# Branches A and B of a hybrid encoder layer: values with v stationary and channels first, probabilities divided by their sum ahead of their transposes

## The reference

```python
def hybrid_layer(x, ...):
    h = rms_norm(x, norm_g)
    proj = jnp.einsum('bsd,de->bse', h, w_in) + b_in          # split into the operands of A, B, C and gates
    y_a = indexer_sparse_attention(a_q, a_k, a_v, i_q, i_k, i_w)   # 8 heads, 2 of k and v, of 64; top 128 keys of an indexer
    y_b = chunked_relpos_attention(b_q, b_k, b_v, rel_bias)        # 8 heads of 64, chunks of 64 tokens, learned bias
    y_c = mlstm_chunkwise(...)                                     # 4 heads of 128
    ...
    branches = jnp.stack([y_a * silu(a_z), y_b * silu(b_z), y_c * silu(c_z)], axis=2)
    y = jnp.einsum('bsnw,nwd->bsnd', branches, w_branch)
    merged = jnp.sum(sigmoid(gates) * y, axis=2)
    return x + jnp.einsum('bsd,de->bse', merged, w_out)
```

```python
p = jax.nn.softmax(s, axis=-1)        # s: scores with mask or bias
o = jnp.einsum('bhqk,bkhd->bqhd', p, v)
```

## Time and profile before

| | |
|---|---|
| Median of three runs | 1332.26 us (1331.98 to 1332.41) |
| Profiled execution, its own time | 1330.72 us |
| Profiled execution, span | 1328.9 us |
| PE busy | 1287.5 us, 97% |
| PE weight loads busy | 1080.2 us, 81% |
| DVE busy | 714.4 us, 54% |
| ACT busy | 621.8 us, 47% |
| POOL busy | 610.0 us, 46% |
| Mean granted clock of TensorE | 0.996 of full |

### The profile page before, as it was taken

The page is one execution under the profiler, slowest core; times in us unless marked ns, Lnnn a source line. Parts: engine busy times, 40 slices in busy tenths (PEclk is TensorE's granted clock), DMA queues, the critical chain, the costliest instruction groups (busy, mean ns, idle before and its releaser), DMA issues.

```text
span 1328.9 us, 19950 instructions
## 1 busy us (share of the span) xinstructions
PE 1287.5 (97%) x6525; PEld 1080.2 (81%) x6525; DVE 714.4 (54%) x1444; ACT 621.8 (47%) x1119; POOL 610.0 (46%) x767
## 2 busy tenths in 40 slices
PE   5999999999999999999999999999999999999997
PEld 3788888888987888887878888888888878888876
DVE  5678888856347112112657897977544532121155
ACT  4444666776444323333344456577754333323332
POOL 3556333342224555545765543334321545455472
PEclk9999999999999999999999999999999999999998
DMA  5322211222132233333142221112213222322321
GB/s 182 144 89 93 95 49 51 77 73 71 34 127 65 83 100 101 95 101 104 66 175 94 96 96 64 48 58 86 64 49 111 80 80 87 103 95 87 103 95 63
DMA packets 37030, 117.39 MB, mean 88 GB/s; under 512 B 4064, under 2 KB 6496, under 8 KB 36448
## 3 DMA queue, kind: packets, MB, share of 16 engines
q1 hardware_dynamic: 34368, 111.37, 25.2%
q10 hardware_dynamic: 2592, 5.11, 1.2%
HBM read 110.18 MB, written 6.29 MB: 88 GB/s over the span
## 4 chain that ended last, share of the span: by engine, by line
PE 81%; DVE 10%; ACT 4%; issue 3%; POOL 1%; DMA 0%; ACTq 0%; DVEq 0%; SPq 0%; POOLq 0%
PE acc L591 65%; PE ps_o L704 4%; PE ps_t L691 3%; DVE score L1179 1%; PE ps_t L682 1%; PE ps_o L711 1%; PE ps_s L661 1%; DVE top L1178 1%; PE ps_s L667 1%; DVE att_c L1311 1%; POOL w_lo L540 1%; DVE ak_s L1152 1%; PE spare L643 1%; ACT prob L937 1%; PE ps_s L675 1%
## 5 line engine op out<-in xcount | busy, mean ns | idle before, releaser
L540 POOL TENSOR_TENSOR w_lo<-w_raw,w_hi 128x256 fp32r<-128x256 f32 x752 | 598.7, 825 | 687.2 <-ACT w_hi L786 687.2
L591 PE MATMUL acc<-h_hi,w_hi 128*128 128x512 f32 x1136 | 454.2, 400 | 0.3 <-ACT w_hi L786 0.3
L591 PE MATMUL acc<-h_lo,w_hi 128*128 128x512 f32 x1136 | 445.4, 392 | 0.0
L591 PE MATMUL acc<-h_hi,w_lo 128*128 128x512 f32 x1136 | 297.1, 395 | 2.1 <-POOL w_lo L540 2.1
L786 ACT ACTIVATE w_hi<-w_raw 128x1024 fp32r<-128x1024 f32 (+1 forms) x212 | 203.9, 962 | 130.8 <-PE acc L591 100.6
L591 PEld LDWEIGHTS acc<-h_hi,w_hi 128*128 128x128 f32 x1136 | 213.8, 188 | 40.8 <-ACT w_hi L786 0.7
L591 PEld LDWEIGHTS acc<-h_lo,w_hi 128*128 128x128 f32 x1136 | 213.8, 188 | 39.6
L591 PEld LDWEIGHTS acc<-h_hi,w_lo 128*128 128x128 f32 x1136 | 208.2, 188 | 43.2 <-POOL w_lo L540 2.9
L1324 DVE SCALAR_TENSOR_TENSOR gated<-prob,acc 128x512 f32<-128x512 f32 x16 | 11.0, 688 | 247.6 <-PE acc L591 247.6
L987 ACT ACTIVATE prob<-acc,par_half 128x512 f32<-128x512 f32 x48 | 33.0, 688 | 148.4 <-PE acc L591 148.4
L937 ACT ACTIVATE prob<-prob,neg_max 128x128 f32<-128x128 f32 (+3 forms) x128 | 70.6, 552 | 19.5 <-DVE neg_max L1214 19.0
(11 more groups left out here) (239 smaller groups left out, 1819.9 us busy)
## 6 DMA issues: line engine op xcount, KB each, us to landing
w_raw<-w_full SPq DMA_DIRECT2D x164, 512.0 KB, 3.4
w_raw<-w_mix SPq DMA_DIRECT2D x48, 256.0 KB, 2.6
x_kept<-xT SPq DMA_DIRECT2D x2, 2048.0 KB, 9.1
rel<-rel ACTq DMA_DIRECT2D x16, 256.0 KB, 2.7
xT<-x_kept SPq DMA_DIRECT2D x2, 2048.0 KB, 9.2
stage<-x SPq DMA_DIRECT2D x4, 512.0 KB, 7.0
out<-stage SPq DMA_DIRECT2D x4, 512.0 KB, 3.0
consts<-consts ACTq DMA_DIRECT2D x1, 640.0 KB, 4.1
```

What stands on the lines that cost most here:

```text
L540: last = pool.tensor_tensor(w_lo[:, slot, part, :], w_raw[:, raw, part, :], w_hi[:, slot, part, :].bitcast(F32), ALU.subtract)
L591: last = pe.matmul(acc[slot][:, :], w[:, slot, k, :], x[:, k, :], start=(i == 0), stop=(i == 3 * nk - 1))
```

## The change

Three edits belong together:

- A new step ("scale", n-1) in each push of A and B, on DVE, after ("exp", n-1): a reciprocal of the item's row sum and a multiplication of its probabilities in place, semaphore `scaled`. ("turn_p", n) on PE waits for `scaled` and no longer for `prob_ready`.
- The value matmuls of A and B take v as the stationary operand (64 columns) and `prob_t` as the moving one (128 columns), so `ps_o` holds 64 channels on partitions by 4 x 128 queries. DVE's part after four items is now a copy: two for A (heads of even and odd number go to the two halves of the partitions), one for B. `att_a` and `att_b` hold channels first.
- z_a and z_b have no transposes and no use of `spare`; DVE reads `att_a` or `att_b` itself and waits for `out_free`.

Branch C is unchanged. The counts of semaphores follow (`SPARE_USES`, `DVE_STEPS`).

```diff
-        for back, kind in (...) if mlstm else ((2, "exp"), (3, "turn_p"), (4, "values")):
+        for back, kind in (...) if mlstm else ((2, "exp"), (2, "scale"), (3, "turn_p"), (4, "values")):
...
-        att = {"a": at("att_a", [P, NT, HEADS * HD], F32, r4), "b": at("att_b", [P, NT, HEADS * HD], F32, r4 + 4 * ROW)}
+        att = {"a": at("att_a", [P, BR, SEQ], F32, r4), "b": at("att_b", [P, BR, SEQ], F32, r4 + 4 * ROW)}
...
 # PE, turn_p
-                            pe.wait_ge(prob_ready, l * ITEMS + n + 1)
+                            pe.wait_ge(scaled, l * 64 + n + 1)
...
 # PE, values
-                                last = pe.matmul(ps_o[:, place * HD:(place + 1) * HD], prob_t[:, n % 2, s * P:(s + 1) * P],
-                                                 v[:, s, f:f + HD], start=(s == 0), stop=(s == t))
+                                last = pe.matmul(ps_o[0:HD, place * P:(place + 1) * P], v[:, s, f:f + HD],
+                                                 prob_t[:, n % 2, s * P:(s + 1) * P], start=(s == 0), stop=(s == t))
...
 # PE, z_a, z_b and z_c
-                    elif kind in ("z_a", "z_b", "z_c"):
+                    elif kind == "z_c":
...
 # DVE
+                    elif kind == "scale":
+                        _, _, t = item(n)
+                        x = prob[:, n % 3, 0:(t + 1) * P]
+                        dve.wait_ge(prob_ready, l * ITEMS + n + 1)
+                        link(dve.reciprocal(row_inv[:, n % 4:n % 4 + 1], row_sum[:, n % 8:n % 8 + 1]))
+                        dve.tensor_scalar(x, x, row_inv[:, n % 4:n % 4 + 1], None, ALU.mult).then_inc(scaled, 1)
...
 # DVE, values
-                            link(dve.reciprocal(row_inv[:, :], row_sum[:, o:o + 4]))
...
-                            dve.tensor_tensor(dst, ps_o[:, 0:4 * HD].rearrange("p (g d) -> p g d", g=4),
-                                              row_inv[:, :].unsqueeze(2).broadcast_to([P, 4, HD]), ALU.mult).then_inc(out_free, 1)
+                            if branch == "a":
+                                pair = ps_o[0:HD, :].rearrange("p (u e q) -> p u e q", u=2, e=2)
+                                u = h // BR * 2
+                                dve.tensor_copy(att["a"][0:HD, u:u + 2, t * P:(t + 1) * P], pair[:, :, 0, :])
+                                last = dve.tensor_copy(att["a"][HD:P, u:u + 2, t * P:(t + 1) * P], pair[:, :, 1, :])
+                            else:
+                                last = dve.tensor_copy(att["b"][h % 2 * HD:(h % 2 + 1) * HD, h // 2, :], ps_o[0:HD, :])
+                            last.then_inc(out_free, 1)
...
 # DVE, z_a and z_b
+                            dve.wait_ge(out_free, l * GROUPS + (8 if kind == "z_a" else 16) + FREE)
+                            inner = att[kind[2]][:, n, :]
```

More of the change, by code:

```diff
@@ L92, in push @@
         mlstm = any(m is not None and m >= 64 for m in flying[-4:])
-        for back, kind in ((1, "exp"), (2, "turn_p"), (3, "values")) if mlstm else ((2, "exp"), (3, "turn_p"), (4, "values")):
+        for back, kind in ((1, "exp"), (2, "turn_p"), (3, "values")) if mlstm else ((2, "exp"), (2, "scale"), (3, "turn_p"), (4, "values")):
             if len(flying) >= back and flying[-back] is not None:
@@ L271, in freed @@
     return l * len(own) + sum(u <= use for u in own)
-SPARE_USE, SPARE_USES = order("turn_iw", "turn_v", "z_a", "z_b", "z_c", "turn_c", "out_gate")
+SPARE_USE, SPARE_USES = order("turn_iw", "turn_v", "z_c", "turn_c", "out_gate")
 SPARE_USES += 2
@@ L280 @@
 STACK_LO, _ = order("iq_lo", "ik_lo", "ak_lo", "aq_lo", "bq_lo", "bk_lo")
-DVE_STEPS = 259
+DVE_STEPS = 307
 def item(n):
@@ L448, in build @@
             sem("evac"), sem("roped"), sem("conv_sum"), sem("conv_tanh"), sem("conv_done"))
+        scaled = sem("scaled")
         small_ready, score_part = sem("small_ready"), sem("score_part")
@@ L713, in _ @@
                         last.then_inc(out_full, 1)
-                    elif kind in ("z_a", "z_b", "z_c"):
+                    elif kind == "z_c":
                         use_spare(l, step)
[L716 to L719, removed]
+                        pe.wait_ge(normed, l * CH + n + 1)
                         for t in range(NT):
@@ L1232, in _ @@
                         if branch != "c":
-                            o = n % 8 - 3
-                            link(dve.reciprocal(row_inv[:, :], row_sum[:, o:o + 4]))
-                            dst = (att["a"][:, t, (h - 3) * HD:(h + 1) * HD].rearrange("p (g d) -> p g d", g=4) if branch == "a"
-                                   else att["b"][:, :, h * HD:(h + 1) * HD])
-                            dve.tensor_tensor(dst, ps_o[:, 0:4 * HD].rearrange("p (g d) -> p g d", g=4),
-                                              row_inv[:, :].unsqueeze(2).broadcast_to([P, 4, HD]), ALU.mult).then_inc(out_free, 1)
+                            if branch == "a":
[6 more added lines that the diff above has]
+                            last.then_inc(out_free, 1)
                         else:
@@ L1255, in _ @@
                         half = par_half[:, C_CNORM + n:C_CNORM + n + 1] if kind == "z_c" else 0.5
-                        dve.wait_ge(spare_full, l * SPARE_USES + SPARE_USE[step] + 3)
-                        dve.scalar_tensor_tensor(gated[:, :], zt, half, spare[:, :], ALU.mult, ALU.mult).then_inc(gated_ready, 1)
+                        if kind == "z_c":
+                            dve.wait_ge(spare_full, l * SPARE_USES + SPARE_USE[step] + 3)
+                            inner = spare[:, :]
+                        else:
+                            dve.wait_ge(out_free, l * GROUPS + (8 if kind == "z_a" else 16) + FREE)
+                            inner = att[kind[2]][:, n, :]
+                        dve.scalar_tensor_tensor(gated[:, :], zt, half, inner, ALU.mult, ALU.mult).then_inc(gated_ready, 1)
                         dve.wait_ge(gated_ready, l * 12 + zn + 1)
-                        dve.sem_inc(spare_free, 1)
+                        if kind == "z_c":
+                            dve.sem_inc(spare_free, 1)
                     elif kind == "y_split":
```

## The result

The changed kernel takes 1405.28 us (1404.56 to 1407.34, 4 runs), the kernel before 1332.12 beside it (1330.23 to 1332.41): a ratio of 1.0555 [1.0537, 1.0573]. It is slower by 73 us, where 22 were predicted, and outside the range. The sign is right, the size is not. In the changed kernel the lines are the passes L592, the scores L662 and L668, the transposes L692, the values L705, the scale L1219 and L1220, the maximum L1212, the exponential L935 and the copies L1240, L1241 and L1243.

The account below looks back on a forecast made before the run. PE, busy 97%, was taken to bound the kernel, with DVE counting where it gates PE. 1330.7 - 7.5 (transposes) + 0 (values) + 30.0 (DVE) = 1353.2, with 1.5 to the median 1354.7 us; range 1338 to 1378.

Parts of the forecast that it names:

- I take 0: Value matmuls on PE: swapping operands changes nothing, as the limit passes from load to moving side at about 0.10 us.
- Bounds: Value matmuls, 640 records: from +5 us for the doubled moving side to -32 us if only the halved load counts.
- rival (b): Value matmuls get cheaper by the halved load, 32 us, about half of it showing: 1339 us; chance 5%.
- The one-column records: Eight PE records with one moving column, 0.10 us apart, said to agree with load time going with stationary columns.
- The scale's instructions: +30: DVE's added scale steps and copies, less its waits for PE: +15.0 us a layer, +30.0 in two layers.
- covered: Items 48 to 63: DVE's added 9.7 us against 14.3 us that it waits for PE, so no cost.
- +0.08 for GpSimd: Scale step on DVE: 0.08 us added per item because such operations grow beside GpSimd.
- The shorter allowance costs up to one push, 2 us a layer: PE's transposes wait for a later scale; set against DVE leaving 282 about as late without PE noticing.
- Rival (c): DVE and ACT block each other, scale waiting for exp behind the gates: 1365 us, 1380 at high price; chance 20%.
- The transposes: -7.5: PE saves 16 groups of four transposes for z_a and z_b at 0.47 us a group: -7.5 us.
- stalls gathered in the gate units: Sign that the forecast is wrong: stalls in the gate units, pointing to DVE and ACT blocking each other.
- (a): Rival: DVE hides the added work and PE keeps its gain, 1325 us; chance 7%.

Follow-up runs that it names:

- f1: e3 with the scale's reciprocal and multiplication added on a scratch tile, DVE waiting for nothing there and PE not waiting for the result; 1356.82 us (ratio 1.0195).
- e3: Changed kernel with stationary v 128 columns wide and no scale, division by the row sums in A and B left out; 1334.24 us (ratio 1.0024).
- e1: Changed kernel, scale kept, with stationary v 128 columns wide in the value matmuls; 1392.02 us (ratio 1.0457).
- f4: e1 with scale, transposes of the probabilities and values each one push later and a fourth slot of prob; 1366.6 us (ratio 1.0275).
- h2: e3 with the 16 groups of four transposes put back in front of the gates of A and B; 1339.62 us (ratio 1.0061).
- g4: f1 with PE's transposes also waiting for DVE's multiplication on the scratch tile; 1371.75 us (ratio 1.0312).
- e2: Changed kernel without the scale, PE waiting for the exponential, division by the row sums left out; 1359.93 us (ratio 1.0216).

## Why the prediction was wrong

**The value matmuls: "I take 0".** This step failed as put. Bounds were set on load time and moving columns, both from records of the full array, and neither bound held the case. The reasoning on the moving side was right: with 128 stationary columns the swapped records take 0.81 us for eight, as before. What it left out is that 64 stationary columns change the shape of the array, and loads don't run ahead across that. The missing term is 0.33 us x 128 items = 42 us on PE; 25.7 of them show without the scale, 13.3 with it. The load did become shorter, 0.137 us in place of 0.191 by the mean, by 28% and not by half, and it bought nothing; rival (b) is refuted. The one-column records could not have agreed with a load that goes with its columns, as the prediction says: all their loads have 128 columns.
The rule of the Trainium skill (TensorEngine Tiling (Array Packing), Tiling Modes, Key Properties) spoke against this change and was not weighed. Nor were the small matmuls of the kernel before at 72.33, whose stop at the change of shape stood in the trace.

**The scale's instructions: +30.** Right that DVE's added work comes through, and the size is near: 22.6 us (f1), copies not among it. Where it comes through was missed: 18.8 us of PE's stalls in f1, against 5.1 in e3, wait for the group's copy out of `ps_o`. Per stretch of layer 0 the time from maximum to maximum grows from e3 to f1 by 8.5, 2.7 and 0.9 us for items 0 to 31, 32 to 47 and 48 to 63; forecast 10.8, 4.2 and "covered". The mean multiplication was dearer than the price, 0.498 us against 0.46 (kernel after: busy us, mean ns, idle before):

```profile
L1219 DVE RECIPROCAL row_inv<-row_sum 128x1 f32<-128x1 f32 x128 | 20.4, 159 | 26.8 <-ACT prob L935 26.4
...
L1220 DVE TENSOR_SCALAR prob<-prob,row_inv 128x512 f32<-128x512 f32 x32 | 19.0, 594 | 1.1
L1220 DVE TENSOR_SCALAR prob<-prob,row_inv 128x256 f32<-128x256 f32 x32 | 18.6, 581 | 1.1
L1220 DVE TENSOR_SCALAR prob<-prob,row_inv 128x384 f32<-128x384 f32 x32 | 16.4, 513 | 1.1
...
L1220 DVE TENSOR_SCALAR prob<-prob,row_inv 128x128 f32<-128x128 f32 x32 | 9.7, 303 | 1.1
```

The medians are 0.288, 0.355, 0.421 and 0.488 us for 128 to 512 columns, as priced before the 0.08 was added. The means are higher because 34 of the 128 took longer than that by more than 0.05 us, and each of these ran beside GpSimd's subtractions (L541); 14 of them happen to have 256 columns, which is why that mean stands out. So +0.08 for GpSimd was +0.11.

**"The shorter allowance costs up to one push, 2 us a layer ... I set them against each other."** This is the second step that failed, and the larger one. The text named both dependences, PE's on DVE and DVE's on ACT, and then booked nothing for them. They cost 35 us with the load (14.9 and 20.3). The error was to price a wait once, at the place where it first bites. By the order of the steps it can come back with every push (this loop is read from the kernel; the runs show its price, not each link): DVE late makes PE late, late scores make the next maximum late, and DVE spends part of the room it had standing for exp. Items 48 to 63, "covered" by 14.3 us of waiting, show it plainest: in layer 0 it is 48.7 us from maximum 48 to 63 in e3, 49.6 with the load (f1), 54.8 with the real scale (e1), 57.1 in the kernel after, against 48.8 before. Room counted as a sum was not room at the moment when PE needed the result. f4, with one push more between the steps, gets 25 of the 35 us back, which fits.

**Rival (c)** had the right mechanism, DVE and ACT blocking each other, at 5 us a layer; the wait of DVE for ACT is worth 10 a layer, and 16.7 of its 26.4 us in the kernel after stand where (c) put them, under items 48 to 63. It was the nearest of all rivals and ended at 1380, 12 us under e1 and 25 under the result.

**The transposes: -7.5.** 5.4 by h2, and not seen in the end, since the swapped form loses 8 elsewhere.

**The signs to look for.** Seen: the stall at item 0 (1.5 us for 1.2), 31.4 us of PE idle behind the multiplication (a little over the 20 to 30), DVE busy 790.4, transposes gone. The 790 is partly luck: the multiplications took 63.7 us, not 49, and the difference was made up by overlaps of neighbouring instructions, which busy time counts once (about 8 us), and by shorter operations elsewhere (about 5). Not seen: DVE's waits for PE near zero under items 0 to 31 (7.0 us in layer 0), and nearly all stalls before item 48 (4.2 of 16.4 us in layer 0 are after it). Of the four signs of being wrong only "stalls gathered in the gate units" pointed the right way; none named a longer stop between array shapes. The chances given to the times add up to 98%, since (a) and (b) share 2%.

**The clock** was no term of the sum. The mean granted clock is 0.985 against 0.996. In the three stretches of 10 us of layer 0 shown above it is 0.83, that is 1.7 us each at most, some 5 us. Layer 1 has more of it: 0.66 and 0.74 in the two stretches shown, 0.84 from 880 to 890 us and 0.90 to 0.99 in four others, some 10 us at most. Part of these 15 us falls into time in which PE waits anyway. No experiment separates the clock from the stalls that precede it. Over the attention of both layers it is 1.00 in e3, 0.99 and 0.98 in f1, 0.97 and 0.99 in g4, 0.98 in e1, so the terms below hold a share of it each.

With hindsight the sum is: 1334.2 (e3) + 22.6 + 14.9 + 20.3 + 13.3 = 1405.3. It is closed by construction, each term being the difference of two runs in this order; in another order the shape change costs 25.7 and the scale 45.4.

## What to carry to other kernels

Before swapping the operands of a small matmul between large ones, look at how many columns become stationary, and look in the old trace for a matmul of another shape and the time that passes around it: one visit to a 64-column shape cost 0.33 us here, whether it held two matmuls or eight, and padding the stationary operand to 128 columns removed it. A step put between two engines has to be priced as a link in a loop, not as load alone: ask how many pushes old its input is and how old its output may get, and give it slack of its own; moving it by one push was worth 25 us here, some three quarters of what its instructions didn't explain. Ask also what else stands on the same queue that another engine waits for: here the copy that empties the one output bank. And find the floor of a plan first: the version with the costly step simply left out (e3) was no faster than the kernel before, so no place for the step could be expected to win while the matmuls and copies stay as they are.

## What the runs showed of the hardware

- Between value matmuls with 64 stationary columns and neighbours with 128, loads of the stationary operand start together with their matmul, 0.2 us late on either side (kernel after: 23.5 us at 117 places, 20.5 us at 114). A visit to the other shape costs 0.33 us of PE's time, for two records or eight (e2 against e3). The kernel before shows the same start of the loads around matmuls of 4 rows, at 72.33 us.
- A multiplication of 128 values in each of 128 partitions by a column takes 0.288 us by the median, one of 512 values 0.488 us (kernel after). Beside GpSimd's subtraction of two tiles in SBUF single ones take up to 0.947 us; all 34 clearly longer ones of 128 ran beside one, but so did 15 that were not longer.
- After stalls of 1.0 and 1.5 us at item 0 of the kernel after, passes started 0.57 and 0.42 us apart in place of 0.23, with a granted clock of 0.83 over those 10 us. After a single stall of 2.1 us at 286.8 us passes started 0.33, 0.24 and 0.23 us apart, with a granted clock of 1.00 from 280 to 290. After 4.4 us of standing still in f1, at 205.46, they started 0.43 us apart.
